# A hybrid decoder step on one core: last head's steps reordered, DeltaNet state reads two slots up, part of the last residual sums on TensorE and ScalarE

## The reference

```python
x = x + rmsnorm_post(W_out @ [mLSTM heads | retention heads | gated DeltaNet heads](W_in @ rmsnorm(x)))
x = x + rmsnorm_post(W_down @ square(relu(W_up @ rmsnorm(x))))       # D_FF = 4 * 2048
# gated delta rule, one of 8 heads of 128, per token
S = exp(g) * (I - beta * k k^T) S + beta * k v^T ;  o = S^T q
# mLSTM, one of 4 heads
m = max(logf + m, i);  C = f' C + i' k v^T;  n = f' n + i' k;  h = q^T C / max(|q.n|, exp(-m))
```

## Time and profile before

| what | value |
|---|---|
| median of three runs | 3106.57 us |
| the profiled execution's own time | 3103.61 us |
| its span | 3102.1 us |
| TensorE busy, matmuls | 3046.1 us (98%) |
| VectorE busy | 1922.9 us (62%) |
| ScalarE busy | 1548.7 us (50%) |
| POOL busy | 85.2 us (3%) |
| HBM traffic | 160 GB/s over the span |

### The profile page before, as it was taken

How to read it: one execution, slowest core, us unless ns; L and a number is a source line. 1 busy time by engine, 2 the same in 40 slices (tenths; PEclk the granted TensorE clock), 3 DMA queues, 4 the chain that set the end, 5 groups by cost and what they waited for, 6 DMA issues and landing times.

```text
span 3102.1 us, 66910 instructions
## 1 busy us (share of the span) xinstructions
PE 3046.1 (98%) x22980; PEld 2977.7 (96%) x22980; DVE 1922.9 (62%) x3992; ACT 1548.7 (50%) x3588; POOL 85.2 (3%) x162
## 2 busy tenths in 40 slices
PE   8999999999999999999999999999999999999998
PEld 7999999998999999999989999999989999999997
DVE  7688886656545545455586888856565454554555
ACT  6577775545434334334455677755453343343343
POOL 1100000000000000000001000000000000000000
PEclk9999999999999999999999999999999999999999
DMA  6544445453444444444445444454444444444444
GB/s 215 190 152 148 142 148 172 154 181 134 165 163 163 166 162 164 170 163 164 153 150 183 144 148 148 148 171 158 162 135 165 161 165 169 160 168 162 163 163 157
DMA packets 267223, 499.89 MB, mean 161 GB/s; under 512 B 34640, under 2 KB 39904, under 8 KB 267040
## 3 DMA queue, kind: packets, MB, share of 16 engines
q1 hardware_dynamic: 244080, 443.58, 43.4%
q0 software_dynamic: 14752, 51.05, 4.6%
q10 hardware_dynamic: 8208, 2.81, 0.4%
HBM read 475.32 MB, written 22.01 MB: 160 GB/s over the span
## 4 chain that ended last, share of the span: by engine, by line
PE 87%; DVE 7%; ACT 2%; issue 2%; DMA 2%; SPq 0%; POOL 0%; ACTq 0%; DVEq 0%; POOLq 0%
PE PU L521 77%; PE PABCD L521 3%; PE PF L521 3%; PE PE_ L521 3%; DVE WL L1338 2%; ACT AE L913 1%; DMA RAW<-in_w 1%; DVE Y L1360 1%; PE PABCD L524 1%; DVE X L1367 1%; ACT WH L913 1%; ACT Y L913 0%; DMA out_sout<-Y 0%; DVE HL L1343 0%; DVE AE L1719 0%
## 5 line engine op out<-in xcount | busy, mean ns | idle before, releaser
L521 PE MATMUL PU<-HH,WH 128*128 128x288 f32 x4000 | 1233.0, 309 | 21.1 <-DVE HL L1343 10.2
L913 ACT ACTIVATE WH<-RAW 128x512 fp32r<-128x512 f32 x1669 | 966.0, 621 | 564.6 <-PE PU L521 461.0
L1338 DVE TENSOR_TENSOR WL<-RAW,WH 128x512 fp32r<-128x512 f32 x1668 | 1075.1, 687 | 264.8 <-ACT WH L913 251.0
L521 PE MATMUL PU<-HH,WL 128*128 128x288 f32 x4000 | 1178.2, 295 | 0.0
L521 PE MATMUL PU<-HL,WH 128*128 128x288 f32 x4000 | 1171.0, 296 | 0.0
L521 PEld LDWEIGHTS PU<-HH,WH 128*128 128x128 f32 x4000 | 753.7, 188 | 47.7 <-issue 29.6
L521 PE MATMUL PU<-UH,WH 128*128 128x288 f32 x2560 | 759.1, 297 | 2.8 <-DVE UL L1504 1.9
L521 PEld LDWEIGHTS PU<-HL,WH 128*128 128x128 f32 x4000 | 750.1, 189 | 9.3 <-issue 3.3
L521 PE MATMUL PU<-UL,WH 128*128 128x288 f32 x2560 | 755.2, 295 | 0.0
L521 PEld LDWEIGHTS PU<-HH,WL 128*128 128x128 f32 x4000 | 755.2, 189 | 0.0
L521 PE MATMUL PU<-UH,WL 128*128 128x288 f32 x2560 | 752.6, 294 | 0.0
(11 more groups left out here) (274 smaller groups left out, 2257.9 us busy)
## 6 DMA issues: line engine op xcount, KB each, us to landing
RAW<-in_w SPq DMA_DIRECT2D x1669, 256.0 KB, 3.7
SIN<-in_sin POOLq DMA_DIRECT2D x32, 512.0 KB, 4.9
out_sout<-Y POOLq DMA_DIRECT2D x32, 512.0 KB, 5.2
BC<-gate_rows POOLq DMA_DIRECT2D x32, 304.0 KB, 4.6
AUX<-in_aux POOLq DMA_DIRECT2D x32, 152.0 KB, 3.9
X<-in_x SPq DMA_DIRECT2D x4, 576.0 KB, 7.1
out_y<-X SPq DMA_DIRECT2D x8, 288.0 KB, 2.1
out_sout<-SOUT ACTq DMA_DIRECT2D x32, 64.0 KB, 2.3
```

Source lines behind the costliest of these rows:

```text
L521: return nc.tensor.matmul(out, lhsT, rhs, start=start, stop=stop, skip_group_check=True)
L913: return nc.scalar.activation(out, in_, f, **kw)
L1338: tt(WL[s % 2][:, k], RAW[c][:], WH[s % 2][:, k].bitcast(F32), ALU.subtract).then_inc(sem("lo_ready"), 1)
```

## The change

The reads' first slot goes from 10 to 8. The last head's steps get another table (squares and NOUT's store in slot 8, sums and then the state product in slot 10, logs, state addition and the rest in slot 11), and for it ScalarE issues the store of the prompt's state behind the squares instead of ahead. At the end, X of groups 5, 6 and 7 is updated by TensorE (identity times X plus identity times Y in free PSUM banks) and ScalarE (the copy back), VectorE scales the groups in another order and adds five of the eight, and SP stores them in a third order. The diff, without its empty lines:

```diff
--- before.py
+++ after.py
@@ -65,7 +65,7 @@
-ROOT_SLOT, INVERSE_SLOT, READ_SLOT = 5, 8, 10
+ROOT_SLOT, INVERSE_SLOT, READ_SLOT = 5, 8, 8
 CONV_SLOTS = (8, 16, 24)
 EXP_AFTER, LOG_AFTER, TAPS_A_SLOT = (4, 4, 3), (6, 6, 4), (1, 1, 2)
@@ -73,13 +73,15 @@
+TAIL = (0, 1, 5, 6, 2, 7, 3, 4)
+BY_PE = (5, 6, 7)
 LINEAR_SLOTS = {0: 3, 1: 4, 2: 8, 3: 18, 4: 20, 5: 21, 8: 24, 9: 25, 10: 26, 11: 27, 12: 28}
 LINEAR_READ = (11, 12, 14)
 RET_SLOTS = {**LINEAR_SLOTS, 2: 6}
 ROTATE_SLOTS, FIRST_ROTATE_SLOTS = (16, 17, 19, 21), (20, 23, 25, 26)
 EARLY_SLOTS, EARLY_READ = {0: 1, 1: 2, 2: 5, 3: 15, 4: 17, 5: 18, 8: 20, 9: 21, 10: 22, 11: 23, 12: 24}, (8, 9, 11)
 LINEAR_DECAY_SLOTS, EARLY_DECAY_SLOTS = (11, 13, 15, 17), (8, 10, 12, 14)
-LAST_SLOTS = {0: 0, 1: 1, 2: 3, 3: 6, 10: 8, 12: 8, 4: 9, 5: 9, 8: 11, 9: 11, 11: 11}
+LAST_SLOTS = {0: 0, 1: 1, 2: 3, 3: 6, 5: 8, 4: 8, 8: 10, 10: 10, 9: 11, 12: 11, 11: 11}
 JOINED = [(0, kk) for kk in range(7)] + [(1, kk) for kk in range(7)] + [(0, 7), (1, 7)] + [divmod(t, 8) for t in range(16, SLOTS)]
@@ -399,9 +401,12 @@
             sp.wait_ge(sem("lo_ready"), 16 * DEPTH * QUADS + 1)
             load(0, 4 * DEPTH * QUADS + 1)
-            for g in range(8):
-                sp.wait_ge(sem("x_updated"), 2 * (16 * DEPTH + g + 1))
+            for g in (0, 1, 5, 2, 6, 3, 7, 4):
+                if g in BY_PE:
+                    sp.wait_ge(sem("tail_copied"), 2 * (BY_PE.index(g) + 1))
+                else:
+                    sp.wait_ge(sem("x_updated"), 2 * (16 * DEPTH + g + 1))
                 k = slice(2 * g, 2 * g + 2)
                 sp.dma_start(d["y"][:, k], X[:, k]).then_inc(sem("y_stored"), 16)
             sp.wait_ge(sem("y_stored"), 16 * 8)
@@ -607,6 +612,25 @@
                 mm(PC[:, 0:T], ONES[:], SQSUM, True, False)
                 pe.wait_ge(sem("output_squares"), 2 * (NC_ * e + NC_ - 1) + 1)
                 mm(PC[:, 0:T], ONES[:], SQ[:, 3], False, True).then_inc(sem("output_summed"), 1)
+            def tail_bank(c):
+                return (PA, PB, PD, PE_, PF, PU[0])[c - 2 * BY_PE[0]][:, 0:T]
+            def tail_sums(l):
+                e = 2 * l + 1
+                chunks = [c for g in BY_PE for c in (2 * g, 2 * g + 1)]
+                pe.wait_ge(sem("psum_read"), 4 * (DEPTH * QUADS - 1) + 5)
+                for c in chunks[0:3]:
+                    mm(tail_bank(c), IDENT, X[:, c], True, False)
+                output_sum(e)
+                for c in chunks[3:6]:
+                    mm(tail_bank(c), IDENT, X[:, c], True, False)
+                for g in BY_PE:
+                    pe.wait_ge(sem("y_scaled"), 9 * e + TAIL.index(g) + 2)
+                    for c in (2 * g, 2 * g + 1):
+                        mm(tail_bank(c), IDENT, Y[:, c], False, True).then_inc(sem("tail_summed"), 1)
             def gate_part(t, kind, l):
@@ -901,7 +925,7 @@
             pe.sem_inc(sem("psum_read"), 2)
             pe.wait_ge(sem("ones_set"), 1)
             walk(pe, None, quad,
-                 lambda l: output_sum(2 * l), lambda l: output_sum(2 * l + 1))
+                 lambda l: output_sum(2 * l), lambda l: output_sum(2 * l + 1) if l < DEPTH - 1 else tail_sums(l))
         @block.scalar
@@ -1124,9 +1148,12 @@
                     act.wait_ge(sem("mls_nout"), 3 * (nk + 1))
                     act.dma_start(d["nout"][bass.ds(nk, 1)].rearrange("a p b -> p (a b)"), NOUT[:]).then_inc(sem("norm_out"), 16)
                 if step == 5:
-                    store_prompt_state(n, l * HEADS + (H_C + H_B if mls else H_C) + hk)
+                    if not last:
+                        store_prompt_state(n, l * HEADS + (H_C + H_B if mls else H_C) + hk)
                     act.wait_ge(sem(f"{kind}_head"), nk + 1)
                     fn(SQH[:], HHD[:], ACT.Square).then_inc(sem("head_squares"), 1)
+                    if last:
+                        store_prompt_state(n, l * HEADS + (H_C + H_B if mls else H_C) + hk)
                 if step == 8:
                     head_log(n)
                 if step == 9:
@@ -1309,6 +1336,9 @@
                 weigh(l, 2, NC_ - 1)
                 if l == DEPTH - 1:
                     hi_part((l + 1) * QUADS, 4)
+                    for i, c in enumerate(c for g in BY_PE for c in (2 * g, 2 * g + 1)):
+                        act.wait_ge(sem("tail_summed"), i + 1)
+                        fn(X[:, c], (PA, PB, PD, PE_, PF, PU[0])[i][:, 0:T]).then_inc(sem("tail_copied"), 1)
             act.sem_inc(sem("head_log"), 1)
             act.wait_ge(sem("ones_set"), 1)
@@ -1359,11 +1389,11 @@
                     dve.wait_ge(sem("output_squares"), 2 * NC_ * (e + 1))
                 tt(Y[:, k], Y[:, k], RS[:].unsqueeze(1).to_broadcast([128, 2, T]), ALU.mult).then_inc(sem("y_scaled"), 1)
-            def add_x(l, which, g):
+            def add_x(l, which, g, place=None):
                 e = 2 * l + which
                 k = slice(2 * g, 2 * g + 2)
-                dve.wait_ge(sem("y_scaled"), 9 * e + g + 2)
+                dve.wait_ge(sem("y_scaled"), 9 * e + (g if place is None else place) + 2)
                 tt(X[:, k], X[:, k], Y[:, k], ALU.add).then_inc(sem("x_updated"), 2)
             def gate_weights(l, j):
@@ -1882,12 +1912,11 @@
                 if l < DEPTH - 1:
                     update_and_split(l, 1, l + 1, 0, NG0, (l + 1) * QUADS)
                 else:
-                    for g in range(8):
+                    for g in TAIL:
                         scale_y(l, 1, g)
-                        if g > 1:
-                            add_x(l, 1, g - 1)
-                    add_x(l, 1, 7)
-                dve.wait_ge(sem("x_updated"), 2 * (8 + 16 * l + 16))
+                        for done in {6: (1,), 7: (2,), 4: (3, 4)}.get(g, ()):
+                            add_x(l, 1, done, TAIL.index(done))
+                dve.wait_ge(sem("x_updated"), 2 * (8 + 16 * l + 16) - (2 * len(BY_PE) if l == DEPTH - 1 else 0))
                 dve.sem_inc(sem("layer_free"), 1)
             for a, v in ((ONES, 1.0), (EPSC, EPS), (ROWA, 0.0), (ROWB, 0.0), (CB0, 0.0), (CUR, 0.0), (COLA, 0.0), (COLB, 0.0), (SMALLS, 0.0), (PMS, 0.0)):
```

## The result

The changed kernel takes 3162.0 us (four runs, 3148.8 to 3163.7) against 3106.05 for the kernel before: a ratio of 1.0174 with an interval of 1.016 to 1.0187, so 56 us slower. The forecast was 3133.9 with a range of 3127 to 3139, so 27 us slower than before. The direction was right and the size half of what came. The profiled execution has a span of 3159.3 us, 57.2 more than before, and its mean granted clock is 0.985 where before it was 0.995.

What follows compares the result with a forecast made beforehand. TensorE was taken as the bound nearly everywhere. Reads +25.5, last head +2.4 and tail -0.6 summed to +27.3 us: 3130.9 against the profiled execution, 3133.9 against the median, range 3127 to 3139.

Steps and rivals of the forecast that it cites:

- The bound: DeltaNet heads: TensorE's queue is the path, busy 228.5 of 230 us, so its waits lengthen the kernel.
- The reads' wait: Sixteen DeltaNet heads: TensorE stands in slot 8 until VectorE has written QKG; +25.5 us, all on the path.
- rival 3: Heads: part of the reads' wait is given back as VectorE and ScalarE catch up; -8, 3126 us; chance 0.06.
- the one on the clock: Heads' waits under 2 us are shorter than the about 3.5 us gap after which TensorE's clock fell in the tail.
- rival 1: Out quad: the clock falls in the gap ahead of the third unit; 1.5 us lost twice, +3, 3137; chance 0.10.
- The last head: Last head, each layer: UL 1.9 us earlier, but a later state store delays the third unit; +1.2 twice, +2.4.
- 5.1 us to landing: Out quad: the state's store, issued at 2156.55, lands at 2161.65, holding the copy into Y and the third unit.
- the state's store isn't late: Out quad: the store lands ahead of the copy, so the last head gains 3.8 us; 3127.7; chance 0.06.
- The tail: Kernel's end: three fewer VectorE adds -2.0, sums of squares later +0.6, last stores queueing +0.8; sum -0.6 us.
- The rival in which VectorE paces the heads: Heads: TensorE's new wait only replaces waits in slots 10 to 19, reads cost 0; 3102.2 us; chance 0.03.

Runs made afterwards that it cites:

- the filled gap: Kernel before with reads from slot 8 and three idle identity products ahead of TensorE's wait in each head: 3129.2 us, ratio 1.0081.
- the wait alone: Kernel before, reads still in slots 10 to 17, but TensorE waits for QKG at the end of its slot 8: 3150.6 us, ratio 1.0153.
- QKG ahead of the mask: Kernel before with reads from slot 8 and VectorE writing QKG at the start of its slot 8, before transpose and mask: 3125.2 us, ratio 1.0077.

## Why the prediction was wrong

The bound was right: in the heads TensorE's queue is the path, and its wait was not given back.

The reads' wait was right in mechanism and size. The prediction summed 16 waits to 28 us and their cost to 25.5; the trace shows 28.2, and the kernel with the filled gap, at full clock, is 25.1 slower. So nothing of the wait was given back, which answers rival 3 too.

The step that failed is the one on the clock: "The waits in the DeltaNet heads, under 2 us, are shorter." From the tail, where the clock fell 3.5 us after the last matmul, I took that a pause has to be of such a length. So I gave the clock a chance of 0.10 in the out quad and none in the heads, and its term there, which came to 34 us, was put at nothing. The trace of before spoke against it, in the second layer's first quad (columns of the earlier trace rows):

```profile
1572.00:1574.00 2.00, 1.05 (x6) 0.82 (x6) 1.83 (x4) 1.32 (x3) 0.00 (x0) 1.00 0.83 205
...
1574.00:1576.00 2.00, 0.72 (x3) 0.58 (x3) 0.92 (x2) 0.11 (x1) 0.00 (x0) 0.81 0.97 366
...
1576.00:1578.00 2.00, 2.00 (x9) 1.86 (x8) 1.12 (x2) 0.52 (x1) 0.00 (x0) 0.50 1.02 384
```

The clock fell at about 1575.25, with TensorE busy for 0.72 of the 2 us of that row and for 1.05 of the 2 before. The longest of TensorE's waits there is this one, from 1573.28 to 1575.28:

```profile
PE PABCD L521 <- DVE Y L1384: 2.0, 1, 2.0
```

No pause of 3.5 us was needed. The rule of the Trainium skill that I cited ("TensorE: Matmul & The Clock Gate", "Why this matters for your kernels") warns of idle gaps between bursts, and names longer ones than these. The runs here agree in kind, and show that in this kernel pauses of 1.8 to 2.0 us, and at times of 1.2 to 1.4, can be enough. By rival 1's own arithmetic, half of the time at the lower level is lost, the 77 us would have given 38, close to the 34 of the matmuls' spacing. But the length of those 77 us could not be had from the rows of before. In the out quad, where I looked for it, the clock stayed at 1.00, and the pause was 1.4 us.

The last head was right up to UL and wrong in the next term, "5.1 us to landing": it landed after 2.9, so the part gains 2.8 us where 2.4 were to be lost. The duration of a transfer was carried over to another moment, though what ran beside it had changed. That was the rival "the state's store isn't late", in part: the copy still waits for it, but for 0.9 us. This error of 5 us hid a part of the other: with the last head right, the forecast would have been further off.

The tail was right in each term (0.57 for 0.6, 1.43 for 1.4 at VectorE's end, 0.7 for 0.6 in sum). The rival in which VectorE paces the heads is refuted: at full clock a wait of 28 us cost 25.

In numbers: forecast 25.5 + 2.4 - 0.6 = 27; found 25 + 34 - 2.8 - 0.7 = 56.

## What to carry to other kernels

Where TensorE is the bound, price a new wait twice: its own length, and the clock behind it. Pauses of nearly 2 us, one in each of sixteen heads, cost about as much by the clock (34 us, and 21 with the wait alone) as by themselves (25). To tell the two apart, fill the pause with idle matmuls: here that took only the clock's share away. A small step that is moved up must be held against the slot in which its input is written on the other engine: slot 9 cost 5 us here, slot 8 cost 56. And take a DMA's duration only together with what is issued beside it.

## What the runs showed of the hardware

- The clock can fall late. In the second head of the changed kernel the pause ended at 233.4, the clock fell at about 234.8 and came back at about 245, all the while with TensorE busy. Behind its ten falls in the heads the delay was 1.0 to 2.1 us. In the first quad of the second layer before, it fell at the end of the pause itself (fall at about 1575.25, pause to 1575.28).
- Of the changed kernel's fourteen waits of 1.77 to 2.00 us the clock fell behind eight, and behind both of those of 1.16 and 1.24 (behind one of the two such waits with the reads alone moved, behind neither with the wait alone). With QKG ahead of the mask it fell behind two of fourteen waits of 1.2 to 1.4 us. With the gaps filled, and waits of 0.5 us at most left, it never fell in the heads.
- A 512 KB store from the POOL queue landed after 5.1 us where two weight loads ran beside it for 1.3 us, after 3.5 with 0.7 us together, and after 2.9 with none.
